# A hybrid block in float32: the serial state chain of the RWKV stage and the modulation sums of the state space stage, issued in another order

## What is computed

```python
def step(state, inp):                    # wkv7_scan, once per token and head, both directions
    r_t, w_t, k_t, v_t, kk_t, kka_t = inp
    sa = einsum('bhvk,bhk->bhv', state, kk_t)
    state = state * w_t - sa[..., None] * kka_t + v_t[..., None] * k_t
    return state, einsum('bhvk,bhk->bhv', state, r_t)

def carry_step(h, inp):                  # ssd_chunked, once per chunk of 128 tokens
    st, dec = inp
    return h * dec[..., None, None] + st, h

mod_x = (silu(c) @ w_mod + b_mod)        # shifts, scales and gates of the norms
```

## Time and profile before

| | |
|---|---|
| median of three runs | 4421.08 us (4410.38, 4421.08, 4421.88) |
| the profiled execution | 4421.88 us, span 4420.1 us, mean granted clock 0.965 |
| front, up to the first Gram block of rwkv | 0 to 195 us |
| rwkv | 195 to 1584 us (steady turns 84 to 91 us each) |
| ssd | 1595 to 2261 us (steady turns 79.7 us each) |
| merge and start of peer | 2277 to 3050 us |
| experts of peer | 3050 to 4420 us |

### The profile page before, as it was taken

How to read it: one execution, slowest core, us unless ns; L and a number is a source line. 1 busy time by engine, 2 the same in 40 slices (tenths; PEclk the granted TensorE clock), 3 DMA queues, 4 the chain that set the end, 5 groups by cost and what they waited for, 6 DMA issues and landing times. The chain is left out here.

```text
span 4420.1 us, 82207 instructions
## 1 busy us (share of the span) xinstructions
PE 3832.9 (87%) x36046; PEld 2392.3 (54%) x36046; DVE 2044.1 (46%) x3468; ACT 742.5 (17%) x1311; POOL 784.5 (18%) x747
## 2 busy tenths in 40 slices
PE   7999999999999879999979999885677777777777
PEld 3466666666666636666568888774222222222223
DVE  1345555555555546776730000113654554554542
ACT  2232223222222212222110000110010111111101
POOL 3000000000000000000000000002545444444431
PEclk9999999999999979999989999997899999999999
DMA  9211111111111046565634444143999999999996
GB/s 379 68 45 45 47 35 47 46 46 47 45 47 35 14 145 206 167 200 167 190 133 152 152 152 161 49 162 129 392 404 419 401 407 419 403 405 420 404 422 254
DMA packets 395487, 868.56 MB, mean 197 GB/s; under 512 B 16604, under 2 KB 228142, under 8 KB 328494
## 3 DMA queue, kind: packets, MB, share of 16 engines
q0 software_dynamic: 73728, 536.90, 29.6%
q1 hardware_dynamic: 229744, 280.60, 19.0%
q10 hardware_dynamic: 91710, 46.43, 3.8%
HBM read 859.68 MB, written 4.19 MB: 195 GB/s over the span
## 5 line engine op out<-in xcount | busy, mean ns | idle before, releaser
L2378 PE MATMUL ps<-vb,diag 128*128 128x512 f32 x2048 | 964.4, 618 | 384.0 <-DMA vb<-in_peer_v,ixv 280.5
L2378 PEld LDWEIGHTS ps<-vb,diag 128*128 128x128 f32 x2048 | 382.5, 195 | 965.9 <-issue 615.6
L2280 DVE SCALAR_TENSOR_TENSOR junk<-ub,hT 128x2048 f32<-128x2048 f32 x256 | 586.9, 2293 | 572.1 <-DMA ub<-in_peer_u,ixu 569.7
L956 PE MATMUL ps<-hT,w_pair 128*128 128x512 f32 (+1 forms) x1536 | 633.7, 540 | 3.3 <-PEq L218 2.2
L1662 PE MATMUL ps<-hT,w_group 128*128 128x256 f32 (+1 forms) x1536 | 512.0, 487 | 0.0
L2183 POOL DMA_INDIRECT vb<-in_peer_v,ixv x256 | 302.1, 1180 | 525.3 <-PE ps L2378 486.7
L1662 PEld LDWEIGHTS ps<-hT,w_group 128*128 128x128 f32 x1536 | 287.2, 190 | 174.2 <-issue 153.6
L956 PEld LDWEIGHTS ps<-hT,w_pair 128*128 128x128 f32 x1536 | 268.1, 190 | 178.6 <-issue 154.9
L2175 POOL DMA_INDIRECT ub<-in_peer_u,ixu x256 | 309.0, 1207 | 208.6 <-issue 99.3
L2346 ACT ACTIVATE diag<-ident,coef 128x128 f32<-128x128 f32 x256 | 101.0, 400 | 1005.0 <-PE ps L2378 994.9
L1867 PE MATMUL ps<-hT,w_merge 128*128 128x256 f32 x1024 | 224.6, 382 | 16.6 <-DMA w_merge<-in_w_in 16.6
(11 more groups left out here) (380 smaller groups left out, 4533.3 us busy)
## 6 DMA issues: line engine op xcount, KB each, us to landing
w_mod_piece<-in_w_mod SPq DMA_DIRECT2D x128, 512.0 KB, 4.8
w_pair<-in_w_in SPq DMA_DIRECT2D x48, 1024.0 KB, 6.1
w_group<-in_w_in ACTq DMA_DIRECT2D x44, 1024.0 KB, 7.2
w_mod_ring<-in_w_mod SPq DMA_DIRECT2D x16, 2048.0 KB, 14.0
w_merge<-in_w_in SPq DMA_DIRECT2D x8, 4096.0 KB, 12.6
w_merge<-in_w_branch_a SPq DMA_DIRECT2D x4, 4096.0 KB, 12.6
w_merge<-in_w_branch_b SPq DMA_DIRECT2D x4, 4096.0 KB, 12.7
w_merge<-in_w_out SPq DMA_DIRECT2D x4, 4096.0 KB, 13.9
```

The source lines that it names most:

```text
L956: last = mm(ps[:, 4, t0:TOK], w[:, m % 2, k, :], hT[:, k, t0:TOK], start=(k == 0), stop=(k == KC - 1))
L2280: nc.vector.scalar_tensor_tensor(junk[:, :], ub[k % NB][:, :], 1.0, h2_rows[:, n, :], ALU.mult, ALU.mult, accum_out=dots[:, k:k + 1]).then ...
L2378: last = nc.tensor.matmul(ps[:, 4 * n + c, :], diag[:, k % 2, :], vb[k % NB][:, c * 512:(c + 1) * 512], start=False, stop=False)
```

## The change

On TensorE in rwkv the four Gram blocks no longer stand in pairs: `chain(1)`, `chain(2)` and `chain(3)` come between them, each with one block of the projection in place of two. From there on every chain step up to 6 stands one place earlier in the list, `chain(7)` stands before the first `crossed`, `chain(8)` before the first `level_e`, and the later ones follow until `chain(14)`, which stands before the last `crossed` and `level_e`. VectorE's list is changed to match: `chain(1)` comes ahead of `masked(0)`, and two more steps than before come ahead of level 1. On VectorE in ssd `mods(4, 8)` now stands ahead of the j = 0 state; the state of j = 1 follows after `mods(8, 10)`, that of j = 2 after `mods(10, 12)`. No instruction is added or removed.

```diff
@@ VectorE, rwkv
+                    chain(1, z)
                     if B:
                         masked(0)
-                    chain(1, z)
+                    chain(2, z)
+                    chain(3, z)
                     if B:
                         masked(1)
-                    chain(2, z)
+                    chain(4, z)
                     if B:                      # xi
...
-                    chain(3, z)
+                    chain(5, z)
                     if B:                      # xe
...
-                    chain(4, z)
+                    chain(6, z)
                     if B:                      # x0
...
-                    chain(5, z)
-                    chain(6, z)
+                    chain(7, z)
+                    chain(8, z)
                     for l in LEVELS:
-                        if l == 1:
-                            chain(7, z)
                         if B:
                             level(l)
-                        if l == 4:
-                            chain(14, z)
-                        else:
-                            chain((8, 10, 12)[l - 1], z)
+                        if l < 4:
+                            chain(7 + 2 * l, z)
                         if B:
                             corrected(l)
...
                         if l < 4:
-                            chain((9, 11, 13)[l - 1], z)
+                            chain(8 + 2 * l, z)
@@ TensorE, rwkv
                     if B:
                         gram(0, 0, i)
+                    piece("k", 0, 1)
+                    chain(1, z)
+                    if B:
                         gram(0, 1, i)
-                    piece("k", 0, 2)
-                    chain(1, z)
+                    piece("k", 1, 2)
+                    chain(2, z)
                     if B:
                         gram(1, 0, i)
+                    piece("k", 2, 3)
+                    chain(3, z)
+                    if B:
                         gram(1, 1, i)
-                    piece("k", 2, 4)
-                    chain(2, z)
-                    if B:
                         ...                    # kt0, at0
-                    piece("k", 4, 5)
-                    chain(3, z)
+                    chain(4, z)
+                    piece("k", 3, 4)
...
                     if B:
                         crossed(0, i)
+                    chain(8, z)
+                    if B:
                         level_e(1, i)
-                    chain(7, z)
-                    piece("k", 8, 10)
-                    chain(8, z)
+                    piece("k", 7, 9)
+                    chain(9, z)
                     if B:
                         level_x(1, i)
+                    piece("k", 9, 10)
...
@@ VectorE, ssd
                     mods(0, 4)
                     if A:
                         conv(0)
+                    mods(4, 8)
                     if B:
                         state("0_0", 0, 0)
                         state("0_1", 0, 1)
-                    mods(4, 6)
+                    mods(8, 10)
                     if B:
                         state("1_0", 1, 0)
                         state("1_1", 1, 1)
-                    mods(6, 10)
+                    mods(10, 12)
                     if B:
                         state("2_0", 2, 0)
                         state("2_1", 2, 1)
                     if A:
                         conv(1)
-                    mods(10, 16)
+                    mods(12, 16)
```

More of the change, by code:

```diff
@@ L1145, in _ @@
                         gram(0, 0, i)
-                        gram(0, 1, i)
-                    piece("k", 0, 2)
+                    piece("k", 0, 1)
                     chain(1, z)
                     if B:
-                        gram(1, 0, i)
-                        gram(1, 1, i)
-                    piece("k", 2, 4)
+                        gram(0, 1, i)
+                    piece("k", 1, 2)
                     chain(2, z)
                     if B:
+                        gram(1, 0, i)
+                    piece("k", 2, 3)
+                    chain(3, z)
+                    if B:
+                        gram(1, 1, i)
                         need(pe, VB, "X4", i - 1)
@@ L1166, in _ @@
                         turned("at1", 7, flat(Ah, 1), i)
-                    piece("k", 5, 6)
-                    chain(4, z)
+                    chain(5, z)
+                    piece("k", 4, 5)
                     if B:
@@ L1173, in _ @@
                         turned("kkt1", 7, KR[:, 1, 0:2, :].rearrange("p f t -> p (f t)"), i)
-                    chain(5, z)
-                    piece("k", 6, 7)
+                    chain(6, z)
+                    piece("k", 5, 6)
                     if B:
@@ L1178, in _ @@
                         turned("vt", 5, v_s, i)
-                    chain(6, z)
-                    piece("k", 7, 8)
+                    chain(7, z)
+                    piece("k", 6, 7)
                     if B:
                         crossed(0, i)
-                        level_e(1, i)
-                    chain(7, z)
-                    piece("k", 8, 10)
                     chain(8, z)
                     if B:
+                        level_e(1, i)
+                    piece("k", 7, 9)
+                    chain(9, z)
+                    if B:
                         level_x(1, i)
+                    piece("k", 9, 10)
                     if A:
                         decay_logit(0, p)
-                    chain(9, z)
+                    chain(10, z)
                     if B:
@@ L1195, in _ @@
                     piece("k", 10, 12)
-                    chain(10, z)
+                    chain(11, z)
                     if B:
@@ L1201, in _ @@
                     piece("k", 12, 13)
-                    chain(11, z)
+                    chain(12, z)
                     if B:
@@ L1206, in _ @@
                     piece("k", 13, 15)
-                    chain(12, z)
+                    chain(13, z)
                     if B:
@@ L1212, in _ @@
                     piece("k", 15, KC)
-                    chain(13, z)
+                    chain(14, z)
                     if B:
```

## The result

The changed kernel takes 4469.8 us (median of four, 4467.1 to 4478.7), the kernel before, measured beside it, 4419.3. The ratio is 1.0127 with an interval of 1.0113 to 1.0141: 50 to 62 us slower, where 26 were forecast. The profiled execution of after has a span of 4478.2 us, 58.1 over that of before.

The account below looks back on a forecast made before the run. Both changed stages were taken as bound by TensorE's list of work, so only its waits count. The terms 22.3 + 12 + 3.8 - 2.5 - 9.6 gave +26, so 4447 us, with 4429 to 4462 for 8 in 10.

Parts of the forecast that it names:

- Four `mods`, 7 x 3.18 = 22.3: In ssd, four steps moved ahead of the j = 0 state lengthen TensorE's wait in seven turns: +22.3 us.
- The clock behind it, 7 x 1.7 = 12, at most 17: In ssd, TensorE's clock falls behind each 4.6 us wait, 1.7 us a turn: +12 us, bounds 0 and 17.
- chain(2) waits 0.54 for VectorE, +3.8: Early in rwkv turns, TensorE's moved chain step waits for VectorE in seven turns: +3.8 us, bounds 0 and 7.5.
- level_x(1) loses 0.18, 14 times, -2.5: In rwkv, F of level 1 starts without a chain step before it: -2.5 us, bound 0.
- No cost of the split: In rwkv, single Gram and projection blocks were counted at 0.66 and 0.95 us; the sum has no term for splitting pairs.
- The packet waits, -9.6: In rwkv, late instruction packets keep fixed landing times while instructions move, so TensorE waits less: -9.6 us together.
- The turn without part A, -3: The rwkv turn with only part B wins 3 us, as more chain steps run beside Gram blocks and transposes.
- the first three: Clock holds in ssd (4435, chance 0.14); rwkv packet waits go (about 4430, 0.13); ssd `mods` are covered (4413, 0.06).
- The fourth, that rwkv gets worse: The late chain step costs every rwkv turn 0.54 us and the packets give nothing: 4460 us, chance 0.12.

Follow-up runs that it names:

- fill_wait: Kernel before with only the change's VectorE order in ssd, plus four more projection blocks on TensorE ahead of the j = 1 state products: 4418.6 us, ratio 1.0005.
- mods_two: Kernel before with two, not four, more `mods` ahead of the j = 0 state in ssd: 4439.4 us, ratio 1.0058.
- late_joined: Kernel before with the change's rwkv order, r's weights loaded after v's transposes, and only TensorE's Gram blocks in pairs again: 4423.2 us, ratio 1.0017.
- late_pad: Kernel before with the change's rwkv order, r's weights loaded after v's transposes, and r's third projection block ahead of `level_x(4)`: 4403.8 us, ratio 0.9976.
- pad_level4: Kernel before with only the change's rwkv order, and r's third projection block moved ahead of `level_x(4)`: 4433.0 us, ratio 1.0032.
- late_weights: Kernel before with r's 1 MB weight load held back until v's projection and transposes are done: 4398.2 us, ratio 0.9954.
- early_state: Kernel before with two fewer `mods` ahead of the j = 0 state in ssd: 4412.4 us, ratio 0.9985.

## Why the forecast was wrong

The sign, the larger half and its place were right; the sum was short by some 30 us (56 for 26). By the forecast's own steps:

- *Four `mods`, 7 x 3.18 = 22.3.* Right: L1697 waits 34.3 for 12.6, +21.7, and fill_wait shows that, the clock aside, next to nothing else comes with it.
- *The clock behind it, 7 x 1.7 = 12, at most 17.* The mechanism was right, the size was off: 7 x 2.55 = 17.9. The price came from rows behind 2.8 us. Behind 4.5 us the low clock costs more (6.9 us at 0.63 of the full rate), and mods_two shows that 2.9 us cost 1.4 to 1.5, and that in every other turn. ssd thus has +39.4 for the 34.3 forecast.
- *chain(2) waits 0.54 for VectorE, +3.8.* Not seen in the fourteen turns, but not wrong in kind: k's first block is 0.32 late for another reason, and single blocks are slower, so that chain(2) comes when the state is there. It came in the turn without part A, as below. When the blocks went back into pairs, the wait came: 0.26 us in a turn of late_joined, and 1.2 us with the mask ahead of chain(1).
- *level_x(1) loses 0.18, 14 times, -2.5.* Right. (VectorE now has eight chain steps ahead of level 1, one more than before and not two.) But the same shift was passed over at level 4: on TensorE chain(14), 0.38 us, no longer stands between `level_e(4)` and `level_x(4)`, which comes before F is ready. That costs 0.39 a turn; late_pad got 0.33 of it back in a turn, and pad_level4 and late_pad 6 us each by their medians.
- *No cost of the split.* This step failed. The durations of a Gram block and of a block of the projection were taken from pairs and used for single ones, and ScalarE's copy of v was not looked for. By the rows of one turn it is 0.97 us. Putting the pairs back gave 0.35 net of a new wait of 0.26 (late_joined). With level 4 that is three quarters or more of the 0.9 us that such a turn has lost with the late weights; of the 1.2 without them, the rest is shown by the rows alone and by no run. Fourteen times 1.19, level 4 and the 0.18 of `level_x(1)` included, is 16.6 us, where the sum had +3.8 - 2.5.
- *The packet waits, -9.6.* This step failed in its assumption, that landings are fixed and only the instructions move. The first packet that starts 3 us or more into a turn starts 6.8 us into it before and 7.2 after (means of the fourteen turns), and in the turn at 1236 us at 7.9 for 3.2, so that a turn without a wait there got 2.91 us, with a fall of the clock behind it. Nor did the new order win waits elsewhere. Over all fourteen turns the issue waits are 26.2 us in before and 22.2 in after; but with the rwkv order of before five traces have 19.4 to 27.5, mean 24.7, and with that of after three have 22.2 to 26.2, mean 24.4. In time, the fourteen turns have +14.3 beside a base of 16.6, so in this pair of traces the packets gave 2.3 and not 6.6; by the means of the same traces (1211.5 and 1229.7 us) the turns have +18.2, and the packets gave nothing. What this pair of traces shows as a gain lies within the spread of equal code.
- *The turn without part A, -3.* The packet waits in it did go, 3.0 us in before and none in after. The step overlooked what stands there in their place: with no projection between the Gram blocks chain(2) comes 1.9 us into the turn, while VectorE still finishes the pair before, and waits 2.22 us for it, the 2.2 in the row of L1053 for Ct above. All kernels with the new rwkv order have this wait there, of 1.7 to 3.3 us. Behind it the clock is low, 0.50 from 1506 to 1511 us, as it was behind the packet wait before (0.53 from 1491 to 1496). It is low once more, 0.66 to 0.83 from 1521 to 1536 us, where before it was 1.00 at the same places of the turn; why was not looked for. From its first Gram block to the outputs of the last turn it takes 89.0 us for 86.7. One pair of traces says little here: with the rwkv order of before this stretch took 79.3 to 86.7 us, with that of after 84.1 to 90.2.

The sum as measured: 21.7 + 17.9 in ssd; in rwkv 16.6 - 2.3 in the fourteen turns, +2.3 in the last and -0.6 in the rest; 2.8 elsewhere; 58 for the profiled executions, against 22.3 + 12 + 3.8 - 2.5 - 9.6. Of the rivals the first three are refuted. The fourth, that rwkv gets worse, came true along with the forecast, by another cause than the chain's late step and by more: its 4460 had 0 for the packets, which is what they gave, and still the small clock term.

What stays open: what sets the start of an instruction packet. late_weights shows that the load matters, late_joined that the order of the stream does without it; neither says where a landing will fall. Open too is why the clock falls behind one wait and holds behind its equal.

## What to carry to other kernels

When an order splits pairs of like blocks, take the durations of single blocks from the trace, and look at every step of every engine that comes sooner: what each of them reads had a due time too. Where TensorE waits for an engine in the middle of dense work, give it more work ahead of the wait, or put the awaited step ahead of optional work on the other engine. Where the clock falls behind the wait, that is worth more than the wait itself (fill_wait: 39 us, where the wait had grown by 22); where it doesn't, it is worth the wait (early_state: 7 us). Where waits have no visible cause and the stream is dense in small products, move the loads near them before moving the instructions.

## What the runs showed of the hardware

- An equal wait need not have an equal price. In ssd the same 2.86 us lowered the clock in every other turn (a group of four in 2.07 or 1.13 us), 1.4 us never, 4.5 us always and at a higher price (2.55 us for 1.4 to 1.5). In rwkv it fell behind 1.87 us in one execution and held behind 1.86 at the same place in another, and within after it fell behind 1.75 and held behind 2.67.
- An issue wait of TensorE can be a late instruction packet. In seventeen traces all of them in the rwkv turns ended 1.1 to 1.7 us after a 16 KB packet of the instruction queue, and such packets started at least 3.2 us apart.
- A 1 MB load on another queue delays the start of instruction packets, from 4.6 to 6.8 us into the turn on the mean, and not their transfer: 9.6 of 16.9 us of issue waits at the Gram blocks, and 5.1 of 5.1 at the transposes, went when it was moved. Taking the space between dense parts away brought 11.7 us back without the load.
- A change of shape between neighbours seems to cost TensorE 0.07 to 0.1 us: 64 small products take 0.73 us alone and 0.66 in a pair, a block of 512 columns 1.03 to 1.06 alone between a block of small products and a chain step, 0.96 in a pair, and 0.96 alone behind a chain step.
